# A transformer block on one core: up blocks with unit 3 rounded first, the square on ScalarE, and turned groups taken by halves

## The reference, cut to what matters

```python
h = rms_norm(x, norm_mix_g[l])
proj = jnp.einsum('bsd,de->bse', h, w_in[l])
...
merged = (g_ret * y_ret + g_att * y_att)
x = x + jnp.einsum('bsd,de->bse', merged, w_out[l])
h2 = rms_norm(x, norm_ffn_g[l])
u = jnp.square(jax.nn.relu(jnp.einsum('bsd,df->bsf', h2, w_up[l])))
x = x + jnp.einsum('bsf,fd->bsd', u, w_down[l])
return rms_norm(x, norm_final_g)
```

## Time and profile before

| | |
|---|---|
| median of 3 runs | 1512.82 us (1511.77 to 1512.90) |
| the profiled execution's own time | 1512.22 us |
| its span, first to last instruction | 1510.3 us |
| TensorE matmuls | 1495.5 us busy, 7008 of them |
| VectorE | 1025.1 us busy |
| ScalarE | 791.1 us busy |
| GpSimd | 39.3 us busy |
| mean granted clock of TensorE | 0.999 of full speed |
| chain that ended last | TensorE 81%, VectorE 12%, issue 3%, DMA 2%, ScalarE 1% |

### The profile page before, as it was taken

How to read it: one execution, slowest core, us unless ns; L and a number is a source line. 1 busy time by engine, 2 the same in 40 slices (tenths; PEclk the granted TensorE clock), 3 DMA queues, 4 the chain that set the end, 5 groups by cost and what they waited for, 6 DMA issues and landing times.

```text
span 1510.3 us, 18941 instructions
## 1 busy us (share of the span) xinstructions
PE 1495.5 (99%) x7008; PEld 1285.5 (85%) x7008; DVE 1025.1 (68%) x1360; ACT 791.1 (52%) x1023; POOL 39.3 (3%) x52
## 2 busy tenths in 40 slices
PE   9999999999999999999999999999999999999998
PEld 7788888888888888888888888888888888888886
DVE  5987987555556777777799877338753586438745
ACT  6555555444444454444444555556555555555553
POOL 0000000000000000000000000000000000000000
PEclk9999999999999999999999999999999999999999
DMA  9644545666655665565765888898888878888783
GB/s 362 209 159 167 188 148 174 207 202 225 220 182 184 197 210 170 192 216 195 248 224 193 249 232 275 250 261 233 232 279 249 255 233 253 257 250 254 230 263 116
DMA packets 154392, 333.93 MB, mean 221 GB/s; under 512 B 5600, under 2 KB 5728, under 8 KB 149856
## 3 DMA queue, kind: packets, MB, share of 16 engines
q1 hardware_dynamic: 149296, 299.61, 58.3%
q0 software_dynamic: 4464, 32.51, 11.6%
q10 hardware_dynamic: 576, 1.06, 0.2%
HBM read 298.55 MB, written 2.10 MB: 199 GB/s over the span
## 4 chain that ended last, share of the span: by engine, by line
PE 81%; DVE 12%; issue 3%; DMA 2%; ACT 1%; SPq 0%; POOL 0%; POOLq 0%; DVEq 0%; ACTq 0%
PE acc L437 78%; DVE buf L1004 6%; DVE wlo L995 3%; DMA raw<-in_w_in 2%; DVE buf L1382 1%; ACT buf L686 1%; PE tps L452 1%; PE pps L479 1%; PE pps L462 0%; DVE kT L1004 0%; DVE qT L1004 0%; PE sps L470 0%; DVE ta_lo L1410 0%; PE tps L580 0%; PE tps L582 0%
## 5 line engine op out<-in xcount | busy, mean ns | idle before, releaser
L672 ACT ACTIVATE whi<-raw 128x1024 fp32r<-128x1024 f32 x542 | 568.8, 1055 | 558.1 <-PE acc L437 553.1
L995 DVE TENSOR_TENSOR wlo<-raw,whi 128x1024 fp32r<-128x1024 f32 x480 | 584.2, 1225 | 367.5 <-ACT whi L672 363.4
L437 PE MATMUL acc<-whi,ta_hi 128*128 128x512 f32 x1308 | 502.7, 384 | 4.3 <-DVE wlo L995 3.8
L437 PE MATMUL acc<-whi,ta_lo 128*128 128x512 f32 x1308 | 495.7, 379 | 0.0
L437 PE MATMUL acc<-wlo,ta_hi 128*128 128x512 f32 x1180 | 447.2, 379 | 0.0
L437 PEld LDWEIGHTS acc<-whi,ta_hi 128*128 128x128 f32 x1308 | 247.1, 189 | 52.3 <-DVE wlo L995 11.0
L437 PE MATMUL acc<-whi,tb_hi 128*128 128x512 f32 x736 | 280.1, 381 | 1.0 <-DVE wlo L995 0.7
L437 PE MATMUL acc<-whi,tb_lo 128*128 128x512 f32 x736 | 278.9, 379 | 0.0
L437 PEld LDWEIGHTS acc<-whi,ta_lo 128*128 128x128 f32 x1308 | 247.2, 189 | 35.1
L437 PEld LDWEIGHTS acc<-wlo,ta_hi 128*128 128x128 f32 x1180 | 223.1, 189 | 30.1 <-issue 0.3
L437 PE MATMUL acc<-wlo,tb_hi 128*128 128x512 f32 x616 | 233.5, 379 | 0.0
(11 more groups left out here) (139 smaller groups left out, 792.1 us busy)
## 6 DMA issues: line engine op xcount, KB each, us to landing
raw<-in_w_in SPq DMA_DIRECT2D x66, 1024.0 KB, 5.2
raw<-in_w_up SPq DMA_DIRECT2D x64, 1024.0 KB, 5.8
raw<-in_w_down SPq DMA_DIRECT2D x64, 1024.0 KB, 6.1
raw<-in_w_gate SPq DMA_DIRECT2D x32, 1024.0 KB, 5.4
low<-raw POOLq DMA_DIRECT2D x31, 1024.0 KB, 8.1
raw<-in_w_att SPq DMA_DIRECT2D x16, 1024.0 KB, 5.0
raw<-in_w_ret SPq DMA_DIRECT2D x16, 1024.0 KB, 5.0
raw<-in_w_out SPq DMA_DIRECT2D x16, 1024.0 KB, 5.2
```

The lines of the kernel that those rows point to most:

```text
L437: last = nc.tensor.matmul(paired(acc[B.parity][:, t, :]), a[:, k, tok], halves_in_turn(b), start=(k == 0 and n == 0), stop=(k == KCH - 1 a ...
L672: nc.scalar.activation(whi[:, s:s + UCH, :], raw[:, u * UCH:(u + 1) * UCH, :], ACT.Copy).then_inc(hi_ready, 1)
L995: V_.tensor_tensor(wlo[:, s:s + UCH, :], raw[:, u * UCH:(u + 1) * UCH, :], whi[:, s:s + UCH, :].bitcast(f32), ALU.subtract).then_inc(lo_re ...
```

## The change

Three things. In the blocks i = 1 to 4 of each q, ScalarE rounds unit 3 ahead of the relu, and VectorE's subtraction of unit 3 stands ahead of the transposes; the square goes from VectorE to ScalarE, behind the relu, with a wait for the relu's end; and the transposes stand in groups of 10, 4 and 2. In the five blocks that turn `merged` and the residual the transposes ahead of units 3, 4 and 5 are 7, 3 and 4 instead of 8, 4 and 2. And every turned group, in all stages, is rounded and subtracted in two halves, with a semaphore `first_half` for the first: TensorE waits for it ahead of unit 6, and for the whole group ahead of unit 7 only.

```diff
@@ TensorE, stage 6 (stages 4 and 5 alike)
                 if first:
                     pe.wait_ge(h2T_ready, 3)
                     gemm(B[0], ta_hi, ta_lo, 0, 6)
+                    pe.wait_ge(first_half, T_STAGE5 + 4)
+                    gemm(B[0], ta_hi, ta_lo, 6, 7)
                     pe.wait_ge(h2T_ready, 4)
-                    gemm(B[0], ta_hi, ta_lo, 6, 8)
+                    gemm(B[0], ta_hi, ta_lo, 7, 8)
...
                     if i == 4:
+                        pe.wait_ge(first_half, q * 4 + (T_STAGE6 + 4))
+                    gemm(B[i], hi, lo, 6, 7)
+                    if i == 4:
                         pe.wait_ge(t_free, q * 4 + (T_STAGE6 + 4))
-                    gemm(B[i], hi, lo, 6, 8)
+                    gemm(B[i], hi, lo, 7, 8)
@@ ScalarE
+            def hi_by_halves(src, dst, g):
+
+                for h in range(2):
+                    nc.scalar.activation(dst[:, ds(g * GCH + h * UCH, UCH), :], src[:, h * UCH:(h + 1) * UCH, :],
+                                         ACT.Copy).then_inc(t_hi, 1)
...
                 for i in range(1, 5):
-                    split(B[i], 0, 3)
+                    split(B[i], 0, 4)
...
-                    scaled_relu(B[i - 1])
-                    split(B[i], 3, 4)
+                    squared_relu(B[i - 1])
                     negated(B[i])
                     split(B[i], 4, 8)
...
-            def scaled_relu(B):
+            def squared_relu(B):
                 scaled(B, buf[0], ACT.Relu, rstd2).then_inc(evacuated[B.parity], 1)
+                act.wait_ge(evacuated[B.parity], B.turn + 1)
+                nc.scalar.activation(buf[0][:], buf[0][:], ACT.Square).then_inc(u_ready, 1)
@@ VectorE
-            def turn_among(B, before, src, ready, n):
+            def turn_among(B, before, src, ready, n, order=((3, 0, 7), (4, 7, 10), (5, 10, 14))):
...
-                for u, n0, n1 in ((3, 0, 8), (4, 8, 12), (5, 12, 14)):
+                for u, n0, n1 in order:
...
+            def lo_by_halves(n, src, hi, lo, g, done):
+                for h in range(2):
+                    at = ds(g * GCH + h * UCH, UCH)
+                    dve.wait_ge(t_hi, n * 2 + (h - 1))
+                    V_.tensor_tensor(lo[:, at, :], src[:, h * UCH:(h + 1) * UCH, :], hi[:, at, :].bitcast(f32),
+                                     ALU.subtract).then_inc((first_half, done)[h], 1)
...
                 for i in range(1, 5):
-                    split(B[i], 0, 3)
-                    square(B[i - 1])
-                    turn_among(B[i], q * 4 + (T_STAGE6 + i - 1), buf[0][:], u_ready, q * 4 + i)
+                    split(B[i], 0, 4)
+                    turn_among(B[i], q * 4 + (T_STAGE6 + i - 1), buf[0][:], u_ready, q * 4 + i, ((4, 0, 10), (5, 10, 14)))
                     lo_from_turned(q * 4 + (12 + i), tb_hi, tb_lo, i - 1)
```

More of the change, by code:

```diff
@@ L240, in build @@
         ret_full, ret_read = sem("ret_full"), sem("ret_read")
-        t_hi = sem("t_hi")
+        t_hi, first_half = sem("t_hi"), sem("first_half")
         hT_ready, retT_ready, h2T_ready = sem("hT_ready"), sem("retT_ready"), sem("h2T_ready")
@@ L595, in stage4 @@
                     gemm(Block(B4 + 1), tb_hi, tb_lo, 0, 6)
+                    pe.wait_ge(first_half, 4)
+                    gemm(Block(B4 + 1), tb_hi, tb_lo, 6, 7)
                     pe.wait_ge(retT_ready, 4)
-                    gemm(Block(B4 + 1), tb_hi, tb_lo, 6, 8)
+                    gemm(Block(B4 + 1), tb_hi, tb_lo, 7, 8)
                 else:
@@ L610, in _ @@
                 if j == 0:
+                    pe.wait_ge(first_half, T_STAGE4 + 4)
+                gemm(Block(B5 + j), tc_hi, tc_lo, 6, 7)
+                if j == 0:
                     pe.wait_ge(t_free, T_STAGE4 + 4)
-                gemm(Block(B5 + j), tc_hi, tc_lo, 6, 8)
+                gemm(Block(B5 + j), tc_hi, tc_lo, 7, 8)
             def stage6(q, first, last=False):
@@ L687, in scaled @@
                 return last
+            def hi_by_halves(src, dst, g):
+                for h in range(2):
+                    nc.scalar.activation(dst[:, ds(g * GCH + h * UCH, UCH), :], src[:, h * UCH:(h + 1) * UCH, :],
+                                         ACT.Copy).then_inc(t_hi, 1)
             def hi_from_turned(turn, dst, g):
                 act.wait_ge(t_full, turn + 1)
-                nc.scalar.activation(dst[:, ds(g * GCH, GCH), :], turned, ACT.Copy).then_inc(t_hi, 1)
+                hi_by_halves(turned, dst, g)
             def hi_from_gained(turn, src, dst, g):
                 act.wait_ge(t_free, turn + 1)
-                nc.scalar.activation(dst[:, ds(g * GCH, GCH), :], src[:].rearrange("p t (k n) -> p (t k) n", n=S),
-                                     ACT.Copy).then_inc(t_hi, 1)
+                hi_by_halves(src[:].rearrange("p t (k n) -> p (t k) n", n=S), dst, g)
             def exps(g, c):
@@ L1043, in gain @@
                 V_.tensor_tensor(dst[:].rearrange("p t (k n) -> p (t k) n", n=S), turned, gsl, ALU.mult).then_inc(t_free, 1)
+            def lo_by_halves(n, src, hi, lo, g, done):
[4 more added lines that the diff above has]
+                                     ALU.subtract).then_inc((first_half, done)[h], 1)
             def lo_from_gained(n, src, hi, lo, g, done):
-                dve.wait_ge(t_hi, n)
-                V_.tensor_tensor(lo[:, ds(g * GCH, GCH), :], src[:].rearrange("p t (k n) -> p (t k) n", n=S),
-                                 hi[:, ds(g * GCH, GCH), :].bitcast(f32), ALU.subtract).then_inc(done, 1)
+                lo_by_halves(n, src[:].rearrange("p t (k n) -> p (t k) n", n=S), hi, lo, g, done)
             def lo_from_turned(n, hi, lo, g):
-                dve.wait_ge(t_hi, n)
-                V_.tensor_tensor(lo[:, ds(g * GCH, GCH), :], turned, hi[:, ds(g * GCH, GCH), :].bitcast(f32),
-                                 ALU.subtract).then_inc(t_free, 1)
+                lo_by_halves(n, turned, hi, lo, g, t_free)
             V_.memset(mix[:, 0, 0:P], 0.0).then_inc(warm, 1)
@@ L1376, in _ @@
                     inverse_rms(ms2_ready)
-            def square(B):
-                dve.wait_ge(evacuated[B.parity], B.turn + 1)
-                V_.tensor_tensor(buf[0][:], buf[0][:], buf[0][:], ALU.mult).then_inc(u_ready, 1)
             def stage6(q, first, last=False):
```

## The result

The changed kernel takes 1502.34 us, median of 4 runs (1502.09 to 1502.48), against 1512.40 of the kernel before (4 runs, 1511.77 to 1512.90). The ratio is 0.9934, with a 95% interval of 0.9916 to 0.9951: faster by 10.1 us, clear of 0.2% either way. The forecast was 1502.9, in a range of 1501.5 to 1507.

The account below looks back on a forecast made before the run. TensorE, busy 1495.5 of 1510.3 us, was bounded by weight loads waiting for VectorE's `wlo`. Gains of 7.3 + 0.53 + 0.72 + 0.50 + 0.86 = 9.9 us took the median from 1512.82 to 1502.9, range 1501.5 to 1507.

Parts of the forecast that it names:

- What bounds the kernel, and what a gap costs: TensorE's weight loads wait for VectorE's `wlo`; 39 late starts after 740 us, 15.1 us, about 0.13 of each free.
- Unit 3's rounding ahead of the relu: Up blocks: relus start 0.95 us later, and VectorE subtracts unit 3 while idle, five us before TensorE wants it.
- Square on ScalarE: Up blocks: square takes 1.06 us after a 0.05 wait for ScalarE's own relu; transposes start 0.8 later than before.
- 10, 4 and 2: Up blocks' transposes: unit 4 subtracted 1.0 us ahead of need, unit 5 with 0.44 us of true slack.
- rival 3: Up blocks: shorter slack from ScalarE's self-wait or a slower Square brings back unit 5's gap, 1507 to 1511; chance 0.08.
- Turned groups by halves: Turned groups: half a rounding 0.622 us, half a subtraction 0.688; some 0.15 us more on each engine, costing nothing.
- the waits at 846, 931, 1099: TensorE gaps of 0.85, 0.38 and 0.56 us; closing them was to give 0.72, 0.25 and 0.43 us.
- the rest near 762: A wait of about 0.2 us expected to remain near 762 us in the profile after.
- The `low` copy: Up blocks: issue moves from 855.99 to about 857.1; landing taken as 8.6 us after issue, at 865.7, before 866.85.
- the rows of 8.0 and 10.3: Profile rows of the `low` copy's landing time after issue: 8.0 us in up blocks, 10.3 in a down block.
- Rivals 1 and 2: Up blocks: `low` copy late and eats the gain, 1510, chance 0.06; or later still and kernel slower, 1530, chance 0.03.
- Rival 4: Turned loops: another TensorE wait grows, two per turn of 0.2 us if exposed, under 1 us, 1503.5; no chance given.

Follow-up runs that it names:

- the run with 10 and 6: Changed kernel with 10 and 6 transposes in the up blocks and none behind unit 5, which is subtracted 0.90 us later: 1509.57 us.
- the run with the copy later: Changed kernel with the negated rounding moved behind the roundings of units 4 and 5, so the `low` copy is issued later: 1519.76 us.

## Why the prediction was right, and where it was off

**What bounds the kernel, and what a gap costs: right.** The whole gain is the late weight loads of the view before: 39 gaps, 15.1 us, of which 0.13 each is free. The free part was an inference from two periods. Other runs bear it out at other lengths of a gap: 0.45 us costs 0.31, 0.57 costs 0.44, and gaps of 0.08 to 0.10 in every up block cost 0.1 us or nothing in a whole run. Without it the sum would have been 15. Of the 0.13 us, 0.03 is no wait at all: a load takes 0.189 us and the next starts 0.216 after it, so each bracket holds that much of the ordinary spacing. A load is early by about 0.10 us.

**Unit 3's rounding ahead of the relu: right, and it is the step that pays.** Forecast 3.36 us from there to the first transpose, measured 3.33. By itself, with the square left on VectorE, it pays the whole gain of the up blocks.

**Square on ScalarE: right in its price, idle in its effect.** 1.06 us and a wait for its own engine of 0.03, where I took 0.05 with 0.31 as the upper end. But the prediction did not say that this edit buys nothing beside the other: on VectorE the square would have started at once behind the relu, 0.17 us dearer against a slack of 0.44. The run with it put back shows that: 1502.26. Only with unit 3 behind would the square's move have paid, 2.6 us.

**10, 4 and 2: right.** Slack of unit 5 0.44 us forecast, one transpose of 0.45 measured as the edge, and rival 3, a shorter slack, ruled out for this kernel. Two transposes more, the run with 10 and 6, show what it would have cost.

**Turned groups by halves: right.** 2.4 us, measured alone at 2.45; the waits at 846, 931, 1099 and their likes are gone, and the rest near 762 is 0.28 us for "about 0.2". Rival 4, the waits of the turned loops, did not come up.

**The `low` copy: issue right, landing wrong in sign.** Forecast 5.4 us from ScalarE's first rounding to GpSimd's issue, measured 5.40. But I took 8.6 us for the landing, between the rows of 8.0 and 10.3, for an overlap of 2.6 us with the load ahead; it is 7.0 (6.9 to 7.8). The failed step is that a load 3.1 us ahead overlaps the copy by 2.6 us. That load lands 2.0 us after the copy's issue and the copy's own data start at 1.4, so it is nearly through by then; and what the copy of before shared the DMA engines with was the load *behind* it, which the change took away. With copy and load in reverse order the 8.0 comes back. The Trainium skill (DMA: Bandwidth & Descriptors, SWDGE vs HWDGE vs iDMA) has each DMA engine take turns between the two queues; I wrote that the 10.3 of the down blocks agrees with it and the 8.0 shows little of it. The table alone would fit the rule in both orders, but the queues do not: while the data of a load that came first were running, the copy had no turn for 3.4 us, and a load that came second moved one packet in 3.7 us. The 10.3 us is a late start too: there the copy's data start 3.5 to 4.0 us after issue, with the load 0.8 ahead. At the scale of one transfer the measurement shows the queues one after the other, and goes before the rule; why the copy gets no turn isn't shown.

**Rivals 1 and 2 are real, but not here.** With the load 0.3 us ahead of the copy, the late copy and its stalls come, and dearer than the 1.7 us a block that I gave it for 11.5: 7.9 us in four blocks, since the clock falls too. What kept the changed kernel from it are the 3.1 us. Of a landing of 10.5 to 12.0 us, 3.4 are the late start of its data. The rest, up to 1.4 us more in three of the four blocks, isn't settled: such a copy also meets the next load (issued at 884.2 in the block shown), but that was not tried by itself.

**Not foreseen:** one down block's copy took 12.2 us and cost a wait of 0.32. That is one wait, 0.2 us of time. It is the same block in every run, the second down block of the first q: its copy took 10.3 us in the kernel before and 11.5 to 12.6 in all the others, and the wait was up to 0.65 us in some, none in others. The cause is open.

The sum was 9.9 us, the spans differ by 9.8, the medians by 10.1. Most of the 0.6 us between forecast and result is the starting point: the forecast took 9.9 off 1512.82, the median of the kernel before at that time, which came to 1512.40 with one run more; from there it would have said 1502.5.

## What to carry to other kernels

When the engine that sets the time is 99% busy, look at the waits of its earliest stage (here the weight loads) and calibrate one such wait against a period that you can read without it; a part of each wait may be free. In a chain of two helping engines, first take out of the late stretch the work whose inputs are there early (here one rounding and its subtraction), before you move work between the engines: the first alone paid all 7.5 us, the second alone 2.6 and beside the first nothing. Such gains do not add up, so try each edit without the other. And when an edit moves the release of a buffer, write down where the transfer that it releases now lies against every other transfer with a deadline.

## What the runs showed of the hardware

- A ScalarE instruction that waits for the one before it on the same engine starts 0.03 us after that one's end (852.75 to 852.78); without the wait two such overlap by 0.1.
- A 1 MB copy with addition issued by GpSimd lands after 6.9 to 7.8 us when hardly any load runs beside its data (changed kernel), and after up to 12.6 us with one on each side (down blocks).
- Its data start 1.4 us after issue with no load's data in the way, 1.9 to 2.4 us with a load issued 2.0 us ahead, 3.5 to 4.2 with one 0.8 us ahead (down blocks of the kernels before and after), 4.8 to 4.9 with one 0.3 us ahead. A load issued 3.1 us behind moves hardly any data until the copy's are through, and the copy's data take 6.2 us instead of 5.2.
- After a wait of 2.30 us TensorE's granted clock was 0.69, then 0.50, then 0.95 in windows of 2 us (the first and the last of them mixed); after waits of 1.59 us and less in the same run, and of 1.71 us in the run with the copy later, it stayed at 1.00.
- Between weight loads that start 0.216 us apart, a gap of 0.45 us costs 0.31 and one of 0.57 costs 0.44; gaps of up to 0.10 cost nothing that can be told.
